# Two-layer decoder trunk: C turned on TensorE, and five steps moved in the order of tiles

## The reference, cut to what matters

```python
# layer 0: x += (u * (tril(W_s) @ layer_norm(v) + b_s)) @ w_out,  u, v = split(gelu(rms(x) @ w_in))
# layer 1: u = rms(x) @ w_in; per group g of 16 channels, 64 complex states p:
lam_bar = exp(lam * dt); b_bar = ((lam_bar - 1) / lam) * b
bu = einsum('blgc,gpc->blgp', u, b_bar)
s = scan(s[t] = lam_bar * s[t-1] + bu[t])
y = einsum('blgp,gcp->blgc', real(s), c_re) - einsum('blgp,gcp->blgc', imag(s), c_im) + d * u
x = x + val * sigmoid(gate),  val, gate = split(gelu(y) @ w_out)
# both layers: x += swiglu(rms(x)); x += sigmoid(rms(x) @ w_gate) * (p @ w_proj)
```

## Time and profile before

| | |
|---|---|
| median of three executions | 2258.43 us (2258.06 to 2260.63) |
| the profiled execution | 2258.06 us, span 2256.1 us |
| TensorE busy | 2234.5 us, 99% of the span |
| VectorE, ScalarE, GpSimd busy | 1439.5, 1021.3, 497.7 us |
| granted TensorE clock | 0.998 of full speed |
| memory traffic | 474.10 MB read, 51.91 MB written, 233 GB/s |

### The profile page before, as it was taken

The page is one execution under the profiler, slowest core; times in us unless marked ns, Lnnn a source line. Parts: engine busy times, 40 slices in busy tenths (PEclk is TensorE's granted clock), DMA queues, the critical chain, the costliest instruction groups (busy, mean ns, idle before and its releaser), DMA issues.

```text
span 2256.1 us, 28323 instructions
## 1 busy us (share of the span) xinstructions
PE 2234.5 (99%) x11250; PEld 1839.5 (82%) x11250; DVE 1439.5 (64%) x1582; ACT 1021.3 (45%) x1233; POOL 497.7 (22%) x469
## 2 busy tenths in 40 slices
PE   9999999999999999999999999999999999999998
PEld 7888778888888888888878888888888888888886
DVE  7878767667675766666657865555555445556665
ACT  5544354444444444445444354444444344444444
POOL 1245325456665544301002100000000000000001
PEclk9999999999999999999999999999999999999999
DMA  8667788888877898887779877677666667767763
GB/s 291 191 205 230 239 261 264 244 247 254 251 243 220 256 263 242 250 255 263 240 240 328 315 214 219 205 215 224 213 213 210 195 195 220 220 213 232 225 214 141
DMA packets 348556, 527.89 MB, mean 234 GB/s; under 512 B 106008, under 2 KB 125352, under 8 KB 347784
## 3 DMA queue, kind: packets, MB, share of 16 engines
q1 hardware_dynamic: 337504, 490.59, 70.9%
q0 software_dynamic: 8320, 30.75, 3.8%
q10 hardware_dynamic: 2600, 4.74, 0.6%
HBM read 474.10 MB, written 51.91 MB: 233 GB/s over the span
## 4 chain that ended last, share of the span: by engine, by line
PE 89%; DVE 5%; DMA 4%; issue 1%; ACT 1%; SPq 0%; ACTq 0%; DVEq 0%
PE PS L1563 57%; PE PS L1569 28%; DVE WLO L1056 2%; DMA HT<-zd 2%; PE PS L1754 1%; DMA ROOTU<-rootd 1%; DMA RAW<-in_ple_w_gate 1%; DMA RAW<-in_gm_w_out 0%; DMA zd<-ZT 0%; PE PS L1594 0%; PE PS L1666 0%; PE PS L1779 0%; DVE Z L1337 0%; DMA rootd<-ROOT 0%; PE PS L1771 0%
## 5 line engine op out<-in xcount | busy, mean ns | idle before, releaser
L1563 PE MATMUL PS<-WHI,OP 128*128 128x512 f32 x6208 | 1540.8, 390 | 4.2 <-ACT WHI L779 3.9
L1056 DVE TENSOR_TENSOR WLO<-RAW,WHI 128x1024 fp32r<-128x1024 f32 x783 | 1022.2, 1316 | 668.5 <-ACT WHI L779 664.7
L1563 PEld LDWEIGHTS PS<-WHI,OP 128*128 128x128 f32 x6208 | 1160.8, 188 | 251.0 <-ACT WHI L779 6.0
L779 ACT ACTIVATE WHI<-RAW 128x1024 fp32r<-128x1024 f32 x783 | 826.1, 1061 | 952.9 <-PE PS L1569 808.5
L1569 PE MATMUL PS<-WLO,OP 128*128 128x512 f32 x3104 | 830.6, 389 | 2.3 <-DVE WLO L1056 2.2
L1569 PEld LDWEIGHTS PS<-WLO,OP 128*128 128x128 f32 x3104 | 582.1, 188 | 125.4 <-DVE WLO L1056 4.3
L763 POOL TENSOR_TENSOR ON<-X,GF 128x1024 f32<-128x1024 f32 x3 | 9.9, 3294 | 945.6 <-DVE X L1405 945.6
L666 POOL TENSOR_TENSOR TA<-BRAW,FAC 128x64 f32<-128x64 f32 x16 | 11.3, 708 | 300.7 <-DMA BRAW<-in_s_b_im 300.7
L1068 DVE TENSOR_TENSOR OP<-HT,OP 128x512 fp32r<-128x512 f32 x50 | 35.3, 747 | 48.0 <-ACT OP L794 48.0
L794 ACT ACTIVATE OP<-HT 128x512 fp32r<-128x512 f32 x50 | 28.8, 624 | 66.5 <-DMA HT<-zd 66.5
L827 ACT ACTIVATE S<-PS,RC 128x512 f32<-128x512 f32 x66 | 41.7, 684 | 32.7 <-PE PS L1569 32.7
(11 more groups left out here) (212 smaller groups left out, 948.1 us busy)
## 6 DMA issues: line engine op xcount, KB each, us to landing
RAW<-in_ffn_w SPq DMA_DIRECT2D x528, 512.0 KB, 4.6
RAW<-in_gm_w_in SPq DMA_DIRECT2D x64, 512.0 KB, 4.8
RAW<-in_ple_w_gate SPq DMA_DIRECT2D x64, 512.0 KB, 5.0
RAW<-in_s_w_out SPq DMA_DIRECT2D x64, 512.0 KB, 5.0
zd<-ZT SPq DMA_DIRECT2D x37, 512.0 KB, 3.9
HT<-zd SPq DMA_DIRECT2D x148, 128.0 KB, 5.5
RAW<-in_gm_w_out SPq DMA_DIRECT2D x32, 512.0 KB, 5.1
RAW<-in_s_w_in SPq DMA_DIRECT2D x32, 512.0 KB, 6.4
```

Source lines behind the costliest of these rows:

```text
L779: A_.activation(hi_of(t), RAW[:, t % RING, :], ACT.Copy).then_inc(hi_ready, 1)
L1056: V_.tensor_tensor(lo_of(t), RAW[:, t % RING, :], hi_of(t).bitcast(F32), ALU.subtract).then_inc(lo_ready, 1)
L1563: T_.matmul(dst[:, th, :], x_part, WHI[:, slot, f], start=first and kk == 0 and part == 0, stop=False)
```

## The change

- The last quad of us is turned on TensorE behind the second tile of out0, not the third.
- `set_up` and `turn_p(0)` stand two tiles earlier (`SET_AT`).
- C is no longer turned by VectorE and through `cd`. TensorE multiplies it with the identity in four groups of 16 matmuls (weights 128x64, 64 moving columns, the two groups' halves of the output side by side) behind the tiles out0 + 12, 16, 20 and 24, and ScalarE copies each result from PSUM to `CT`, in a new layout, with the sign of the imaginary part. GpSimd waits for the group it needs. SyncE issues five transfers fewer.
- At the end of gate0 VectorE does `moments` after the quad's `low`; ScalarE takes the root after the quad and behind end+5, not end+2. The store of the root follows that, and its load stands behind end+6, not end+5.
- In win and out1 `INTO_AT` and `OUT_AT` are two tiles earlier (the last output three), and with them the table loads of the pairs after the first two or three. `U_AT` stays.

```diff
-quads("us", range(NT), 16, None, 2)
+quads("us", range(NT), 16, None, 1)
...
-CT_AT = start("out0") + 11
+CT_AT = [start("out0") + 12 + 4 * r for r in range(4)]
-SET_AT = start("v", 1) + 2
+SET_AT = start("v", 1)
...
-INTO_AT = [W0 + 8 * (d // 2) + 16 + d % 2 for d in range(DUOS)]
-OUT_AT = [W0 + 8 * (d // 2) + 20 + 2 * (d % 2) for d in range(DUOS - 2)] + [W0 + 44, W0 + 46]
+INTO_AT = [W0 + 8 * (d // 2) + 14 + d % 2 for d in range(DUOS)]
+OUT_AT = [W0 + 8 * (d // 2) + 18 + 2 * (d % 2) for d in range(DUOS - 2)] + [W0 + 42, W0 + 43]
...
-TQ_AT += [(W0 + g, W0 + g + 1) for g in (17, 19, 25, 27, 33, 35)]
-TD_AT += [(W0 + g, W0 + g + 1) for g in (21, 29, 31, 37, 39)]
-TK_AT += [(W0 + g, W0 + g + 1) for g in (23, 31, 33, 39, 41)]
-TE_AT += [W0 + g for g in (20, 21, 28, 29, 36, 37)]
+TQ_AT += [(W0 + g, W0 + g + 1) for g in (15, 17, 23, 25, 31, 33)]
+TD_AT += [(W0 + g, W0 + g + 1) for g in (19, 27, 29, 35, 37)]
+TK_AT += [(W0 + g, W0 + g + 1) for g in (21, 29, 31, 37, 39)]
+TE_AT += [W0 + g for g in (18, 19, 26, 27, 34, 35)]
...
-        CX = f_view("CX", [P, 2, 2, 2, KB, CH], 8)
-        CT = f_view("CT", [P, QP, 2, KB, CH], 0)
+        CT = f_view("CT", [P, 2, PAIRS, CH], 8)
...
@@ SyncE @@
-            loads_to(CT_AT + 8)
-            sp.wait_ge(cx_ready, 1)
-            sp.dma_start(cd[:, :, :], CX[:, :, :, :, :, :].rearrange("p g s r b c -> p (g s) (r b c)")).then_inc(cd_out, 16)
-            loads_to(CT_AT + 11)
-            sp.wait_ge(cd_out, 16)
-            for i in range(4):
-                sp.dma_start(CT[32 * i:32 * i + 32, :, :, :, :].rearrange("p q r b c -> p q (r b c)"),
-                             cd.rearrange("(q s) i n -> i s q n", q=QP)[i]).then_inc(ct_ready, 16)
...
@@ GpSimd @@
-                if b == 0:
-                    pool.wait_ge(ct_ready, 64)
-                c = lambda ri: CT[:, :, ri, b, :].unsqueeze(3).to_broadcast(shape)
+                if b % 4 == 0:
+                    pool.wait_ge(ct_ready, b // 4 + 1)
+                c = lambda ri: CT[:, ri, pairs, :].unsqueeze(3).to_broadcast(shape)
...
@@ ScalarE @@
+            def turn_c(r):
+                until(CT_AT[r] + 1)
+                act.wait_ge(ct_done, r + 1)
+                for ri in range(2):
+                    last = A_.activation(CT[:, ri, 4 * QP * r:4 * QP * (r + 1), :].rearrange("p q c -> p (q c)"),
+                                         PS[:, 6, 256 * ri:256 * ri + 256], ACT.Copy, scale=(-1.0 if ri else 1.0))
+                last.then_inc(ct_ready, 1)
+
+            turned_c = 0
+            for n in range(1, NT + 1):
+                while turned_c < 4 and CT_AT[turned_c] <= end("out0", n - 1) + 1:
+                    turn_c(turned_c)
+                    turned_c += 1
+                quad_of("out0", n - 1, 1)
+            while turned_c < 4:
+                turn_c(turned_c)
+                turned_c += 1
...
-                    if n == NT - 1:
-                        until(end(stage, n) + 2)
-                        root(i)
-                        act.wait_ge(root_ready, i + 1)
-                        for h in range(2):
-                            act.dma_start(rootd[h].unsqueeze(1), ROOT[:, h:h + 1]).then_inc(root_out, 16)
-                    quad_of(stage, n, 2)
+                    if last:
+                        quad_of(stage, n, 2)
+                if last:
+                    until(end(stage, NT - 1) + 5)
+                    root(i)
...
-            until(end("gate0", NT - 1) + 5)
+            act.wait_ge(root_ready, RMS["win"] + 1)
+            for h in range(2):
+                act.dma_start(rootd[h].unsqueeze(1), ROOT[:, h:h + 1]).then_inc(root_out, 16)
+            until(end("gate0", NT - 1) + 6)
             act.wait_ge(root_out, 32)
...
@@ VectorE @@
-            def turn_c():
-
-                until(CT_AT)
-                dve.wait_ge(c_in, 32)
-                for s_ in range(2):
-                    last = V_.transpose(CX[:, :, s_, :, :, :].rearrange("p g r b c -> p (r b) g c"),
-                                        CN[:, :, :, 32 * s_:32 * s_ + 32].rearrange("p r b x -> p (r b) x"))
-                step(last)
-                im = CX[:, :, :, 1, :, :].rearrange("p g s b c -> p (g s) (b c)")
-                V_.tensor_scalar(im, im, -1.0, None, ALU.mult).then_inc(cx_ready, 1)
...
                     gated(stage, n, PS[:, 6:8, :])
-                    if n == NT - 1:
-                        moments()
                     quad_of(stage, n, 2)
+                moments()
...
@@ TensorE @@
+            def turn_c(r):
+                if r == 0:
+                    pe.wait_ge(c_in, 32)
+                    pe.wait_ge(z_ready, Z_COUNT["us", NT - 1])
+                else:
+                    pe.wait_ge(ct_ready, r)
+                for ri in range(2):
+                    for i in range(4):
+                        for g in range(2):
+                            at = 4 * QP * CH * ri + QP * CH * i
+                            last = T_.matmul(PS[ST * g:ST * g + ST, 6, at:at + QP * CH], CN[:, ri, 4 * r + i, :],
+                                             IDENT[:, :].rearrange("p (q g c) -> p q g c", g=2, c=CH)[:, :, g, :],
+                                             start=True, stop=True)
+                last.then_inc(ct_done, 1)
```

More of the change, by code:

```diff
@@ L353, in trunk @@
         ud = nc.dram_tensor("ud", (P, 2 * NW), F32).ap()
-        cd = nc.dram_tensor("cd", (P, 4, 2 * KB * CH), F32).ap()
         rootd = nc.dram_tensor("rootd", (2, P), F32).ap()
@@ L400, in trunk @@
         c_in = sem("c_in")
-        cx_ready = sem("cx_ready")
-        cd_out = sem("cd_out")
+        ct_done = sem("ct_done")
         ct_ready = sem("ct_ready")
@@ L890, in _ @@
             quad_of("us", NT - 1, 1)
-            for n in range(NT):
-                quad_of("out0", n, 1)
+            def turn_c(r):
[14 more added lines that the diff above has]
+                turned_c += 1
             until(end("out0", NT - 1) + 4)
@@ L923, in downs, with gates @@
                 root(i)
-            def gates(stage, i):
+            def gates(stage, i, last=True):
                 for n in range(NT):
@@ L1369, in residuals @@
                     quad_of(stage, n, 1)
-                    if stage == "out0" and n == 0:
-                        turn_c()
                 moments()
@@ L1663, in taps @@
                     pe.wait_ge(exp_ready, b)
+                else:
+                    pe.wait_ge(ct_ready, 4)
                 for ri in range(2):
@@ L1723, in first_layer @@
                         mix(n)
+                for r in range(4):
+                    if t == CT_AT[r]:
+                        turn_c(r)
             for n in range(1, NT):
```

## The result

| | before | changed |
|---|---|---|
| median of four executions each | 2259.53 us (2258.06 to 2262.49) | 2282.77 us (2281.97 to 2284.14) |
| the profiled execution | 2258.06 us, span 2256.1 | 2284.6 us, span 2282.2 |
| TensorE busy | 2234.5 us | 2247.0 us |

The ratio is 1.0102 with an interval of 1.0085 to 1.0119: the change makes the kernel slower by about 23 us. I had forecast slower, but 2268.7, with 2261.5 to 2276 as the range. The two spans differ by 26.1.

A forecast was written before the change was run, and what follows sets the result against it. TensorE, busy for all but 22 us of the span, was taken to bound the kernel. The terms 2.6 + 1.5 - 3.7 + 3.5 + 3.3 + 3.4 = +10.6 on 2258.1 gave 2268.7 us, range 2261.5 to 2276.

The forecast's parts named there:

- Set-up: Set-up transposes two tiles earlier: TensorE waits for VectorE's copy at 38.6, +2.6 us (+1.3 to +4).
- Quad of us: Last quad of us one tile earlier: TensorE waits until VectorE finishes Z, +1.5 us (1.0 to 2.5).
- C: C turned by TensorE: gaps from 249 to 298 vanish, -7.1; four groups cost 3.4; net -3.7 us (-0.3 to -5.1).
- Root: Last norm of layer 0: root stored 7.7 us later, half of it charged, +3.5 us (-0.5 to +7.7).
- My first rival (root trips hidden): Root's store and load together take less than about 10 us, giving +2.6, 2260.7 us; chance 0.06.
- First pair of state matmuls: State matmuls two tiles earlier: TensorE waits for UP, landing at about 1173.7, +3.3 us (2.5 to 4.2).
- Later pairs: Third, fifth and seventh state matmuls: UP comes after TensorE, +1.0 each and 0.4 for a table load, +3.4 us (0 to 7).

The follow-up runs named there:

- tk_late: The kernel before with the third pair's two TK table loads behind W0+15 and W0+16 instead of W0+4 and W0+6; ratio 0.9977, -5.2 us.
- states_only: The kernel before with only INTO_AT, OUT_AT and the state-space table loads two tiles earlier; ratio 1.0098, +22 us.
- u_early: The changed kernel with U_AT one tile earlier for the second to fourth column; ratio to the kernel before 1.0033, +7.5 us.
- keep_busy: The changed kernel with 30, 20, 52 and 36 identity transposes filling TensorE's waits for UP; ratio to the kernel before 1.0084, +19 us.
- set_busy: The kernel before with set_up and turn_p two tiles earlier and 24 identity transposes ahead of the wait for VectorE's copy; ratio 1.0009, +2.0 us.
- c_tk_late: The kernel before with C turned on TensorE and the third pair's two TK loads moved later; ratio 0.9961, 2252.59 us.

## Why the prediction was wrong in its size

The sum was +10.6; the spans show +26.1. Two steps of the prediction failed where it matters: the path of U in the later pairs (12.0 us of waits where it had 3.4), and the clock behind a wait, which it put at nothing (8.0). Term by term, in its order:

- **Set-up, +2.6.** The wait is right: 2.8 us, on VectorE's copy, ending at 38.63. What failed is that nothing was added for the time behind it: the tile at 39.76 takes 4.4 us instead of 2.8. Measured +4.2.

```profile
38.63 0.37 PE L1612 MATMUL PS<-IDENT,AN 64*128 64x64 f32 x3 [2.81 <-DVE AN L1170]
...
39.76 3.20 PE L1553 MATMUL PS<-WHI,OP 128*128 128x512 f32 x8
```

- **Quad of us, +1.5.** Right: 1.48 us of wait for Z, with the earlier trace rows the row of before, and no fall of the clock behind it.

```profile
208.12 1.06 PE L1584 MATMUL PS<-IDENT,Z 128*128 128x128 f32 x8 [1.48 <-DVE Z L1341]
```

- **C, -3.7.** The -7.1 is right: no gap is left between 246 and 300, where the kernel before had 2.20 and 1.74 us and smaller ones. The price of a group is not: each takes 1.17 us between its tiles and 0.13 behind, 1.30 and not 0.85, as the starts 236.27, 240.16 and 243.02 say. I had counted 16 matmuls a group from the code and compared them with the 64 and 16 that the trace counts for `into_states` and `taps`. But the trace counts 32 here: it lists each of these float32 matmuls twice, so the code's number and the trace's must not be mixed. Two smaller slips: 0.85 does not lie between its two neighbours (16 x 0.03 + 0.3 = 0.78, and 0.84), and 64 transposes at 0.1 make 6.4, not 6.9. Measured by the tiles: -7.1 + 5.2 = -1.9.

```profile
236.27 1.98 PE L1553 MATMUL PS<-WHI,OP 128*128 128x512 f32 x8
...
239.08 1.15 PE L1660 MATMUL PS<-IDENT,CN 128*64 128x64 f32 x32
...
240.16 2.11 PE L1553 MATMUL PS<-WHI,OP 128*128 128x512 f32 x8
...
243.02 1.98 PE L1553 MATMUL PS<-WHI,OP 128*128 128x512 f32 x8
```

- **Root, +3.5.** Wrong; about -0.6. The store came as late as I said: 1145.06 after 1133.30 is 11.8, of which 4.1 are the shift of everything before it, so 7.7. But ROOTU was back 4.5 us after its issue at 1154.62. Halving the 7.7 still charged part of the store's lateness to a trip that was long by its company: the table loads, as tk_late shows, and perhaps the weight loads. My first rival (root trips hidden), with a chance of 0.06, was nearer, though the store alone still took 9 us: the two together took 14.1 us, not less than 10. And the Trainium skill's 2 us a transfer (DMA: Bandwidth & Descriptors, Anatomy of one DMA) is shown by neither trip; the section gives it for transfers that GpSimd issues, and these are ScalarE's.

- **First pair of state matmuls, +3.3.** Right: 3.33 us for UP. The closeness is in part luck: the same steps gave 2.4 in states_only and 1.3 in u_early.

```profile
1170.06 2.67 ACTq L969 DMA_DIRECT2D UP<-ud  x4
...
1177.49 3.63 PE L1764 MATMUL PS<-UP,TQ 128*64 128x32 f32 x64 [3.33 <-DMA UP<-ud]
```

- **Later pairs, +3.4.** This is the step that failed, with the clock. T is again the end of a pair's first state matmuls. The chain was right up to UT, which is ready 14.8 us after T, as I had it (14.6). From there I took the upper end of the landings of before, so that UP would be there at T + 29.3. It came at T + 32.5, 35.3 and 32.9 (T is 1181.1, 1216.4 and 1255.4): `ud` took 7.1, 9.4 and 5.6 us, and from the first issue of UP to the matmuls it was 10.6, 11.1 and 12.4, where I had 7.4. TensorE was there at T + 28.9 to 30.2, where I had 28.3. The waits were 2.3, 5.7 and 4.0, so 12.0 instead of 3.4. I had read the landings in a stretch where U ran ahead of the tables, and moved U's chain against the tables without asking what it would then share the memory with.

- **The lower clock, not in the sum.** 8.0 us behind the four waits of the state-space part. It is a share of the account and not what a steady clock would save: keep_busy got back 3.2 of it by the tiles.

Together: 10.6 + 1.6 (set-up) + 1.8 (C) - 4.1 (root) + 8.6 (later pairs) + 8.0 (clock) = 26.5, against 26.1 between the spans. The direction was right because the waits that I named are there; the range failed because its upper end stacked no more than two bad terms, and because one price, the clock behind a wait, was missing from every term. The root's 4.1 us, wrong the other way, hid part of the miss.

## What to carry to other kernels

Where TensorE is busy for 99% of the span, a wait of a few microseconds can cost more than its length: add what the work behind it takes at the lower clock, or fill the wait. When a consumer is moved ahead, write out the whole chain that feeds it, with the queue order on each engine; here taking one scan from ahead of a transpose was worth about 15 us. A transfer's time depends on its company: read it again for the place to which a change moves it, and look whether the company can be moved instead, as the two table loads could for 5 us.

## What the runs showed of the hardware

- A wait of 2.34 us already brought the granted clock down (0.81 over 1212 to 1221), one of 1.48 us (at 208.12) did not. Between them it went either way. Behind waits of 2.1 and 2.2 us at W0+9 the next tile took 2.86 us in the changed kernel and 4.32 in u_early. In keep_busy one of 1.7 us, behind filled time, was followed by a clock of 0.53 from 1250.5 to 1252.5. In set_busy 24 small transposes in the wait kept it at 1.00 from 36 to 48.
- A small scattered load (ROOTU) took 4.5 to 5.7 us from issue to use while the weight loads paused (seven runs with the root moved), 8.9 to 9.2 beside the weight loads (c_tk_late, tk_late), and 13.7 to 15.0 with two table loads as well (the five runs with neither moved).
- The trace counts a float32 matmul of the C groups twice: 16 in the code, 32 in the trace.
